# Asking for the down weights of a mixture of experts from ScalarE's queue instead of SyncE's

## The reference

```python
def swiglu(x, wg, wu, wd):
    return (jax.nn.silu(x @ wg) * (x @ wu)) @ wd

def route(xf, w_router, router_bias):              # top 8 of 64 for every token
    ...
def moe_ffn(x, ...):                               # x: 256 tokens x 1024
    top_idx, top_w = route(xf, w_router, router_bias)
    y = routed_experts(xf, top_idx, top_w, w_gate, w_up, w_down) \
        + swiglu(xf, ws_gate, ws_up, ws_down)
```

## Time and profile before

| what | value |
|---|---|
| median of 3 runs | 1216.45 us |
| the profiled execution, its own time | 1216.77 us |
| its span, first to last instruction | 1214.7 us |
| TensorE busy | 1180.3 us, 97% |
| ScalarE busy | 262.5 us, 22% |
| moved by SyncE's queue | 451.22 MB, 88.4% of the 16 DMA engines' time |

### The profile page before, as it was taken

The page is one execution under the profiler, slowest core; times in us unless marked ns, Lnnn a source line. Parts: engine busy times, 40 slices in busy tenths (PEclk is TensorE's granted clock), DMA queues, the critical chain, the costliest instruction groups (busy, mean ns, idle before and its releaser), DMA issues.

```text
span 1214.7 us, 17941 instructions
## 1 busy us (share of the span) xinstructions
PE 1180.3 (97%) x7776; PEld 561.6 (46%) x7776; DVE 350.7 (29%) x1070; ACT 262.5 (22%) x513; POOL 10.4 (1%) x20
## 2 busy tenths in 40 slices
PE   7999999999999999999899999999999999999994
PEld 6774544444444444444386655344444444444431
DVE  0434622222222222222343346222222222222224
ACT  1132322211222112221112323122211222212210
POOL 0000000000000000000000000000000000000001
PEclk9999999999999999999999999999999999999998
DMA  9971399999999999999997415999999999999992
GB/s 384 423 306 74 120 399 429 427 427 426 428 427 427 426 428 425 429 426 425 422 384 308 191 35 233 400 428 427 427 427 427 427 427 429 426 425 427 428 427 114
DMA packets 35927, 452.45 MB, mean 372 GB/s; under 512 B 3969, under 2 KB 4097, under 8 KB 6785
## 3 DMA queue, kind: packets, MB, share of 16 engines
q1 hardware_dynamic: 35840, 451.22, 88.4%
HBM read 450.15 MB, written 1.05 MB: 371 GB/s over the span
## 4 chain that ended last, share of the span: by engine, by line
PE 90%; DMA 7%; DVE 2%; ACT 1%; issue 0%; POOL 0%; POOLq 0%
PE bank L616 34%; PE bank L642 17%; PE bank L536 8%; DMA slots<-in_w_gu 6%; PE bank L561 5%; PE bank L715 5%; PE bank L787 4%; PE bank L724 2%; PE bank L628 2%; PE bank L913 1%; PE bank L734 1%; PE bank L583 1%; PE bank L744 1%; PE bank L548 1%; PE bank L820 1%; PE bank L670 1%
## 5 line engine op out<-in xcount | busy, mean ns | idle before, releaser
L642 PE MATMUL bank<-slots,low 128*32 128x512 f32 x2048 | 233.0, 595 | 2.3 <-issue 2.3
L616 PE MATMUL bank<-slots,low 128*64 128x512 f32 x1024 | 226.5, 594 | 2.2 <-DMA slots<-in_w_gu 2.2
L616 PE MATMUL bank<-slots,xT 128*64 128x512 f32 x1024 | 226.1, 594 | 1.0 <-ACT xT L952 1.0
L1228 DVE SCALAR_TENSOR_TENSOR yparts<-bank,small,yparts 128x512 fp32r<-128x512 f32 x128 | 96.1, 751 | 249.1 <-ACT yparts L952 249.1
L536 PEld LDWEIGHTS bank<-high,low 128*128 128x128 bf16 x1536 | 108.2, 147 | 50.4 <-issue 49.7
L616 PEld LDWEIGHTS bank<-slots,low 128*64 128x64 f32 x1024 | 69.1, 137 | 132.2 <-issue 127.6
L616 PEld LDWEIGHTS bank<-slots,xT 128*64 128x64 f32 x1024 | 69.3, 137 | 130.6 <-issue 129.3
L952 ACT ACTIVATE yparts<-bank,small 128x512 fp32r<-128x512 f32 x128 | 88.0, 687 | 157.9 <-PE bank L642 157.9
L1220 DVE TENSOR_TENSOR high<-high,bank 128x256 f32<-128x256 f32 x64 | 26.9, 421 | 327.1 <-ACT high L974 327.1
L536 PE MATMUL bank<-high,low 128*128 128x128 bf16 x1536 | 117.7, 227 | 0.3
L642 PEld LDWEIGHTS bank<-slots,low 128*32 128x32 f32 x2048 | 60.8, 109 | 121.1 <-issue 117.1
(11 more groups left out here) (128 smaller groups left out, 668.2 us busy)
## 6 DMA issues: line engine op xcount, KB each, us to landing
slots<-in_w_gu SPq DMA_DIRECT2D x128, 2048.0 KB, 23.9
slots<-in_w_dn SPq DMA_DIRECT2D x64, 2048.0 KB, 23.2
slots<-in_dense SPq DMA_DIRECT2D x30, 1024.0 KB, 15.2
slots<-in_first SPq DMA_DIRECT2D x4, 768.0 KB, 8.0
r<-in_pool_mat SPq DMA_DIRECT2D x2, 1024.0 KB, 24.0
r<-in_ln_g SPq DMA_DIRECT2D x4, 512.0 KB, 4.5
r<-in_ln_b SPq DMA_DIRECT2D x4, 512.0 KB, 5.5
slots<-in_shared_dn SPq DMA_DIRECT2D x2, 1024.0 KB, 4.8
```

What stands on the lines that cost most here:

```text
L616: m = pe.matmul(H[64 * a:64 * a + 64, :], xg[B % 2][:, k, j, a, :], GU[g][:, a, :, k, :], start=k == 0, stop=k == KD - 1)
L642: m = pe.matmul(Y[half][r0:r0 + 32, :], hT[:, kc * P + 64 * a + 32 * t:kc * P + 64 * a + 32 * t + 32], DN[g][:, a, kc, half * 512:(half + ...
L1228: dve.scalar_tensor_tensor(ysp[:, 1, half * 512:(half + 1) * 512], Y[half][:, :], wslot[:, b:b + 1], ysp[:, 0, half * 512:(half + 1) * 512 ...
```

## The change

SyncE's `run` keeps gu0 and gu1 and loses the wait on `y_full` and the request for dn. ScalarE's `body` of pair q asks for dn of pair q + 3 behind its second copy of Y. The slot, the source, the size and the semaphore of the transfer stay as they were. Dn of pairs 0, 1 and 2 stays with SyncE, as do the further rounds' first three pairs.

```diff
@@ SyncE, run/body
                     load_gu(ps, l, q, g, (0,))
                     sp.wait_ge(ps.h_full, n - 2)
                     load_gu(ps, l, q, g, (1,))
-                    sp.wait_ge(ps.y_full, 2 * (n - 2))
-                    load_dn(ps, l, q, g)
@@ ScalarE, run/body
                         act.wait_ge(ps.y_full, 2 * n + half + 1)
                         copy(ysp[:, 0, half * 512:(half + 1) * 512], Y[half][:, :], scale=wslot[:, b:b + 1])\
                             .then_inc(ps.hi_rd, 1)
+                    if q + 3 < PAIRS:
+                        act.dma_start(slots[:, g, 2 * W_CHUNK:], w_dn[l * PAIRS + q + 3]).then_inc(ps.w_in[2][g], 16)
```

## The result

The changed kernel takes 1233.43 us (median of 4 runs, 1232.13 to 1234.37) against 1216.75 us in the same comparison: ratio 1.0134, 95% interval 1.0122 to 1.0146, or 16.7 us slower. The forecast was 1234. The profiled execution took 1232.13 us, its span is 1230.0 us.

A forecast was written before the change was run, and what follows sets the result against it. PE sets the pace at 13.86 us a pair, but the weight stream, at 14.87, uses up the reserve by the last pair. The profiled 1216.77 + 2 x 8.7 = 1234.2, less 0.32 to the median, gave 1234 us, range 1224 to 1246.

The forecast's parts named there:

- (1): SyncE loses 58 requests and 58 waits; gu0 and gu1 go out when they did: 0.
- (2): ScalarE gains 58 requests of 0.33 us, covered by its idle time before the next silu: 0, at most 19 us.
- (3): Dn requests go out 0.8 us later behind ScalarE's copy (bounds 0 and about 1.5), moving each layer's stream end 0.8 us.
- (4): Expert stage: dn in its own queue overtakes waiting gu, PE waits from about pair 20 to 22: 8.7 us a layer.
- (5): Layer 1's first mixer weights, behind layer 0's expert stage: no wait there to win back, nothing lost.
- (A): Rival: no overtaking, dn keeps its place and is only 0.8 us late: 1218 us, chance 0.08.
- (B): Rival: two queues fill gaps between transfers and the stream gets faster: 1214.6 us, chance 0.07.
- (C): Rival: the stream gets slower while two queues alternate: 1243 us for 1%, chance 0.14.
- (D): Rival: dn is always served first, 12.7 us a layer: 1242 us, chance 0.06.
- (E): Rival: dn gets under a third of the engines and PE waits for dn: from 1240 us upwards, chance 0.03.

The follow-up runs named there:

- loads held back: Kernel before, with all gate, up and down requests of pairs 3 to 31 on ScalarE, and layer 1's first loads waiting for layer 0's last dn: 1219.34 us, ratio 1.0021.
- the last experiment: Kernel before, all requests on SyncE in the old order, dn of pair 3 asked for in two column halves, the first sooner: 1216.00 us against 1216.43, ratio 0.9996.
- the all-ScalarE kernel: Kernel before, with gu0, gu1 and dn of pairs 3 to 31 all asked for from ScalarE in the old order: 1226.62 us, ratio 1.0076.
- the one with 8 KB rows: Changed kernel, with each dn asked for as two 1 MB transfers with 8 KB rows instead of one with 16 KB rows: 1229.76 us, ratio 1.0107 to the kernel before.

## Why the prediction was right

**(1) Nothing from SyncE's lost requests, (2) nothing for ScalarE's.** Right. With 174 requests on ScalarE and its order kept, at most 2.4 us were lost in all (loads held back).

**(3) The request 0.8 us late, the stream's end with it.** Wrong, at the lower bound that I gave. ScalarE hands on the copy and asks at once; both start at the same moment:

```profile
552.12 0.69 ACT L950 ACTIVATE yparts<-bank,small 128x512 fp32r<-128x512 f32 x1 [0.97 <-PE bank L640]
552.12 0.33 ACTq L982 DMA_DIRECT2D slots<-in_w_dn  x1
```

Dn of pair 3 was asked for 13.27 us after pair 0's start (170.44 - 157.17), and 13.25 before. The stream's end did not move in layer 0 and came 0.5 us later in layer 1 (above); since the request was not late, that 0.5 us has another cause, which is not shown. The term was 0, not 1.6 us for both layers. Its premise was weak too: the 6.0 us step at dn of pair 3 also stands deep in the queue (the last experiment).

**(4) Dn overtakes, gu pays.** Right in mechanism, place and size. Expected was gu1 of pair 30 landing two transfers before the end; it landed 594.8 - 585.0 = 9.8 us before it. Expected were waits from pair 20 to 22 at the middle of H; the first is in pair 21 of both layers. Gu1 of pair 16 took 34.1 us to land for 24.3, 9.8 us more, where 9.9 was forecast for two passing dns. Its time levelled off at 40 to 42 us, a little above the 38 to 40 expected. From pair 0 to pair 31, with the old wait of 1.19 us counted in, layer 0 took 586.49 + 1.19 - 158.56 = 429.1 us and now takes 594.55 - 157.17 = 437.4: 8.3 us more for 8.7 expected. In layer 1 the two ends are

```profile
762.67 7.09 PE L614 MATMUL bank<-slots,xT 128*64 128x512 f32 x32 [0.51 <-ACT xT L950]
...
1200.47 7.06 PE L614 MATMUL bank<-slots,low 128*64 128x512 f32 x32
```

437.8 us instead of 1183.90 + 1.03 - 755.99 = 428.9: 8.9 us more. The sum of 17.1 is close to the 17.4 of the forecast. A little of that closeness is luck: without the 0.8 us of (3), which did not come, the same sum is 7.9 us a layer and 15.8 in all, and 1.3 us came from elsewhere, 0.5 of them with the later end of layer 1's stream. The profiled execution's span grew by 15.3 only, since its mixer of layer 0 happened to end 1.4 us sooner (pair 0 at 157.17 instead of 158.56), which the change doesn't touch; by the medians it is 16.7.

The time of a dn was mis-sized: about 9.9 us, or 10 to 13 with what lies around it, was forecast and 14.4 is the median. The turns take about 10 us, as forecast; the 3.5 us before the first packet and the 1 us after the last are what I had too small. It changed nothing in the sum, because gu1 of pair 30 lands two transfers before the end either way.

**(5) Nothing at the seam of the layers.** Right for this change. But the all-ScalarE kernel shows that I had read the seam as a place where only time matters. Its loads are a third party in the stream, and lose or win by the queue they stand in.

**The rivals.** (A) no overtaking is out by the landing times and the packets. (B) and (C), another rate: it was 426 for 427 GB/s, and the end of the stream is the same within 0.1 us in layer 0 and 0.5 us in layer 1. (D) dn always first is out by the half-and-half packets. (E) was not this kernel, but the one with 8 KB rows.

## What to carry to other kernels

Where a stream of loads is as slow as the engine that consumes it, the order of landing decides. Putting a part of that stream into a second queue gave no bandwidth here (426 for 427 GB/s), but let that part pass everything that waited. What passed early in a stage was free while the reserve lasted. What passed when the reserve was nearly spent cost about its own length even as a single transfer: 5.7 us a layer for one of 4.96 us. Before a request is moved to another queue, compare how long each transfer takes to land with how long before its use it is asked for, and look at what else stays in the old queue.

## What the runs showed of the hardware that was not expected

- A request in a queue with no data left to move waited about 3.5 us for its first packet while the other queue was deep (asked at 447.57, first packets at about 451), beside the 10 us of its transfer. Dn of pair 3, asked for at 170.44 when little else was outstanding, moved its first packets at about 172.1, after 1.7 us. Why the deep queue costs more is not shown.
- The two queues got equal numbers of packets and not of bytes, in each of the three pairings seen: 16 KB against 16 KB and against 8 KB rows (above), and this one. In the all-ScalarE kernel, from 574 to 590 us, the mixer weights with rows of 8 KB and less (q1) had 345 packets for 1.85 MB, the expert weights with 16 KB rows (q10) 343 for 4.95 MB:

```profile
q10 hardware_dynamic: 343, 4.95, 72.8%
q1 hardware_dynamic: 345, 1.85, 28.0%
```

- A wait on PE can cost more than itself. After the waits of 2.87, 2.24 and 2.03 us in the all-ScalarE kernel, 16 matmuls took 5.35, 5.35 and 5.33 us instead of 3.65. The windows of that kernel (us, busy by engine, clock, DMA share, GB/s) show a granted clock of 1.00, the level of 2.4 GHz, ahead of the first of these waits, where PE had been busy 3.93 of 4.00 us. Over the wait and the matmuls behind it the mean is 0.76, and inside them it is 0.50, the level of 1.2 GHz:

```profile
572.00:576.00 4.00, 3.93 (x24) 1.12 (x20) 1.73 (x7) 0.69 (x1) 0.00 (x0) 1.00 1.01 418
578.00:585.00 7.00, 6.19 (x24) 2.14 (x24) 0.38 (x1) 0.38 (x1) 0.00 (x0) 0.76 1.00 424
579.30:582.60 3.30, 3.30 (x10) 0.98 (x8) 0.00 (x0) 0.00 (x0) 0.00 (x0) 0.50 1.01 427
```

The length of the wait alone does not tell. In the kernel whose last four dns overtake, the wait of 1.70 us was followed by slow matmuls (5.34 us for 32 instead of 3.64) and the wait of 2.45 us was not. A slow stretch is lost time only where no later wait takes it up, as at the last of the three waits above. In the changed kernel the waits are 1.5 us at most and the matmuls behind them keep their 3.65 us, so its loss has no such part.
